# The recurrent block's join on pairs of tiles, output tiles copied by ScalarE, and a norm's squares summed by TensorE

## The reference

```python
def rmsnorm(x, g):
    y = xf * lax.rsqrt(jnp.mean(xf * xf, axis=-1, keepdims=True) + RMS_EPS)
    return (y * g).astype(x.dtype)

for i in range(DEPTH):                       # DEPTH = 2
    a = rmsnorm(h, g[0])
    m = retention_mixer(a, ...) if i % 2 == 0 else rglru_mixer(a, ...)
    h = h + rmsnorm(m, g[1])
    f = conv_ffn(rmsnorm(h, g[2]), ...)
    h = h + rmsnorm(f, g[3])

def rglru_mixer(h, ...):
    gate, xr = jnp.split(h @ w_in, 2, axis=-1)
    xr = dwconv(xr, conv_w, conv_b, LRU_CONV_LEFT)
    y = (rglru_one_direction(xr, ..., False) + rglru_one_direction(xr, ..., True))
    y = y * jax.nn.gelu(gate)
    return y @ w_out
```

## Time and profile before

| | us |
|---|---|
| median of three runs | 717.61 |
| the profiled execution, its own time | 717.85 |
| its span on the profile | 716.0 |
| TensorE busy (matmul) | 704.6 |
| VectorE busy | 607.3 |
| ScalarE busy | 520.2 |
| GpSimd busy | 25.0 |

### The profile page before, as it was taken

One profiled execution on the slowest core, in us unless ns is written; L12 is line 12 of the kernel. 1 busy time (PEld: TensorE's weight loads), 2 busy tenths in 40 slices (PEclk: granted clock), 3 DMA queues, 4 the chain that ended last, 5 costly groups with the idle time before them and its releaser, 6 DMA issues.

```text
span 716.0 us, 16121 instructions
## 1 busy us (share of the span) xinstructions
PE 704.6 (98%) x6542; PEld 589.9 (82%) x6542; DVE 607.3 (85%) x820; ACT 520.2 (73%) x848; POOL 25.0 (3%) x28
## 2 busy tenths in 40 slices
PE   9999999999999999999999999999899999999996
PEld 6788787878899888888889998888788888885464
DVE  6969877777889799989898889898999999999643
ACT  7566675857576789778777677899668888988431
POOL 0010010101010000000002300000000000000000
PEclk9999999999999999999999999999999999999999
DMA  9873363452683356555589963100525666766821
GB/s 309 318 234 120 119 235 119 166 188 104 211 274 121 111 192 225 192 195 200 176 264 388 370 216 117 62 1 1 196 98 190 224 206 207 233 211 207 275 43 59
DMA packets 106396, 132.08 MB, mean 184 GB/s; under 512 B 12385, under 2 KB 74337, under 8 KB 106209
## 3 DMA queue, kind: packets, MB, share of 16 engines
q1 hardware_dynamic: 105904, 130.97, 54.4%
q10 hardware_dynamic: 432, 0.31, 0.2%
HBM read 129.17 MB, written 1.05 MB: 182 GB/s over the span
## 4 chain that ended last, share of the span: by engine, by line
PE 82%; DVE 8%; ACT 6%; DMA 2%; issue 1%; SPq 1%; DVEq 0%
PE ps L1653 22%; PE ps L1655 22%; PE ps L1654 22%; PE ps L2036 3%; PE ps L2037 3%; PE ps L2035 3%; DMA stage<-in_ret_w_in 2%; PE ps L1696 1%; PE ps L1700 1%; PE ps L1695 1%; DVE a_lo L1082 1%; SPq L495 1%; PE ps L1901 1%; DVE hT L1098 1%; DVE w_lo L1036 1%
## 5 line engine op out<-in xcount | busy, mean ns | idle before, releaser
L1653 PE MATMUL ps<-a_hi,w_hi 128*128 128x272 f16 (+1 forms) x1000 | 276.9, 277 | 0.1
L1654 PE MATMUL ps<-a_lo,w_hi 128*128 128x272 f16 (+1 forms) x1000 | 276.9, 277 | 0.0
L1655 PE MATMUL ps<-a_hi,w_lo 128*128 128x272 f16 (+1 forms) x1000 | 276.9, 277 | 0.0
L1036 DVE SCALAR_TENSOR_TENSOR w_lo<-stage,w_hi 128x1024 f16<-128x1024 f32 x207 | 246.5, 1221 | 34.3 <-ACT w_hi L579 34.0
L579 ACT ACTIVATE w_hi<-stage 128x1024 f16<-128x1024 f32 x207 | 208.5, 1044 | 30.6 <-PE ps L2037 18.3
L1653 PEld LDWEIGHTS ps<-a_hi,w_hi 128*128 128x128 f16 x1000 | 97.8, 98 | 17.3 <-DVE rs L1045 0.9
L1655 PEld LDWEIGHTS ps<-a_hi,w_lo 128*128 128x128 f16 x1000 | 97.8, 98 | 16.0
L1654 PEld LDWEIGHTS ps<-a_lo,w_hi 128*128 128x128 f16 x1000 | 97.8, 98 | 15.7
L1653 PE MATMUL ps<-y_hi,w_hi 128*128 128x272 f16 (+3 forms) x496 | 106.1, 242 | 0.0
L1654 PE MATMUL ps<-y_lo,w_hi 128*128 128x272 f16 (+3 forms) x496 | 106.1, 242 | 0.0
L1655 PE MATMUL ps<-y_hi,w_lo 128*128 128x272 f16 (+3 forms) x496 | 106.0, 242 | 0.0
(11 more groups left out here) (278 smaller groups left out, 1104.2 us busy)
## 6 DMA issues: line engine op xcount, KB each, us to landing
stage<-in_ffn_w_in SPq DMA_DIRECT2D x96, 512.0 KB
stage<-in_ffn_w_out SPq DMA_DIRECT2D x24, 1024.0 KB
stage<-in_ret_w_in SPq DMA_DIRECT2D x16, 1024.0 KB
stage<-in_ret_w_out SPq DMA_DIRECT2D x8, 1024.0 KB
stage<-in_lru_w_in SPq DMA_DIRECT2D x8, 1024.0 KB
stage<-in_ret_w_in SPq DMA_DIRECT2D x12, 512.0 KB
stage<-in_lru_w_out SPq DMA_DIRECT2D x8, 512.0 KB
stage<-in_lru_w_a SPq DMA_DIRECT2D x8, 256.0 KB
```

Of the source, the lines that this page charges most:

```text
L1036: dve.scalar_tensor_tensor(out=part(1, c, q), in0=flat(stage, c, q), scalar=W_SCALE, in1=part(0, c, q), op0=ALU.mult, op1=ALU.subtract).th ...
L1653: pe.matmul(o, w_h, x_h, start=start, stop=False)
L1654: pe.matmul(o, w_h, x_l, start=False, stop=False)
L1655: return pe.matmul(o, w_l, x_h, start=False, stop=stop)
```

## The change

It has three parts.

First, ScalarE now copies all eight output tiles of the recurrent block with their gain from PSUM into `mT` (`out_scaled`), between and behind the squares. VectorE's `out_scale` for tiles 0 and 1 is gone there. `mean_part` waits for the first of these copies (`m_part`) where it waited for `m_scaled`.

Second, `residual` takes its tiles in plain order and in groups: tile 0, tile 1, then the pairs (2, 3), (4, 5), (6, 7). One VectorE instruction multiplies a whole group by the root, one adds it to h. The low parts are still made tile by tile, behind the addition of the next group. `norm_input` and `chunk_normed` follow in plain order.

Third, in the join before the recurrent block (`residual_parts` with i = 1), VectorE stops its sums of squares with four tiles left (0, 1, 4, 5), and TensorE multiplies all four with the ones in `mean_input`.

```diff
-JOIN_ORDER = (2, 3, 0, 1, 4, 5, 6, 7)
+GROUPS = ((0, 1), (1, 1), (2, 2), (4, 2), (6, 2))
...
             def norm_input(i, t0, weights_after=()):
-                for n, dt in enumerate(JOIN_ORDER):
-                    act.wait_ge(h_new, (i - 1) * DT + n + 1)
+                for dt in range(DT):
+                    act.wait_ge(h_new, (i - 1) * DT + dt + 1)
                     high(i, dt, t0)
...
+            def out_scaled(half, n):
+
+                act.activation(mT[:, half * 4 + n, T0_LRU_OUT:T], ps[:, (X, Y)[half] + n, T0_LRU_OUT:T], ACTF.Copy,
+                               scale=gain(5, half * 4 + n)).then_inc(m_part, 1)
+
             out_squares(LRU_OUT + 1, 2, 0, T0_LRU_OUT, 2)
-            out_squares(LRU_OUT + 1, 2, 1, T0_LRU_OUT)
+            out_scaled(0, 0)
+            out_scaled(0, 1)
+            out_square(LRU_OUT + 1, 2, 1, 0, T0_LRU_OUT)
+            out_scaled(0, 2)
+            out_square(LRU_OUT + 1, 2, 1, 1, T0_LRU_OUT)
+            out_scaled(0, 3)
+            out_square(LRU_OUT + 1, 2, 1, 2, T0_LRU_OUT)
+            out_square(LRU_OUT + 1, 2, 1, 3, T0_LRU_OUT)
+            for n in range(3):
+                out_scaled(1, n)
             estimate(STAT, T0_LRU_OUT, ms_up, MEAN[("post", 2)], ESTIMATE[("post", 2)])
+            out_scaled(1, 3)
             norm_input(3, T0_LRU_OUT, (4, 6))
...
             def out_scale(i, t0):
-                for dt in range(4 if i < 2 else 2):
+                for dt in range(4):
...
             def residual_parts(i):
...
-                mark(dve.tensor_tensor(two, two, sq[:, 2:4, :], ALU.add))
+                added = mark(dve.tensor_tensor(two, two, sq[:, 2:4, :], ALU.add))
                 part_low(i, 1, 3)
+                after(added)
                 dve.wait_ge(h_sq, (i + 2) * DT)
-                link(dve.tensor_tensor(four, four, sq[:, 6:8, :], ALU.add))
-                link(dve.tensor_tensor(two, two, four, ALU.add))
-                dve.tensor_tensor(sq_sum[:], sq[:, 0, :], sq[:, 1, :], ALU.add).then_inc(sum_h, 1)
+                if i == 1:
+                    dve.tensor_tensor(four, four, sq[:, 6:8, :], ALU.add).then_inc(sum_h, 1)
+                else:
+                    link(dve.tensor_tensor(four, four, sq[:, 6:8, :], ALU.add))
+                    link(dve.tensor_tensor(two, two, four, ALU.add))
+                    dve.tensor_tensor(sq_sum[:], sq[:, 0, :], sq[:, 1, :], ALU.add).then_inc(sum_h, 1)
...
             def residual(i, t0):
                 rsqrt(rs, STAT, t0, ESTIMATE[("post", i)])
-                dve.wait_ge(m_scaled, i + 1)
-                for n in range(DT + 1):
-                    if n < DT:
-                        dt = JOIN_ORDER[n]
-                        to = mT[:, dt, t0:T]
-                        if dt < 2:
-                            link(dve.tensor_tensor(to, to, rs[:, t0:T], ALU.mult))
-                        else:
-                            link(dve.scalar_tensor_tensor(out=to, in0=ps[:, (X, Y)[dt // 4] + dt % 4, t0:T],
-                                                          scalar=gain(2 * i + 1, dt), in1=rs[:, t0:T],
-                                                          op0=ALU.mult, op1=ALU.mult))
-                        dve.tensor_tensor(hT[:, dt, t0:T], hT[:, dt, t0:T], to, ALU.add).then_inc(h_new, 1)
-                    if n:
-                        norm_low(i + 1, n - 1, JOIN_ORDER[n - 1], t0)
+                for g in range(len(GROUPS) + 1):
+                    if g < len(GROUPS):
+                        dt, count = GROUPS[g]
+                        some = slice(dt, dt + count)
+                        dve.wait_ge(m_part, i * DT + dt + count)
+                        link(dve.tensor_tensor(mT[:, some, t0:T], mT[:, some, t0:T],
+                                               rs[:, t0:T].unsqueeze(1).to_broadcast([P, count, T - t0]), ALU.mult))
+                        dve.tensor_tensor(hT[:, some, t0:T], hT[:, some, t0:T], mT[:, some, t0:T],
+                                          ALU.add).then_inc(h_new, count)
+                    if g:
+                        before_dt, count = GROUPS[g - 1]
+                        for dt in range(before_dt, before_dt + count):
+                            norm_low(i + 1, dt, dt, t0)
...
-            out_scale(2, T0_LRU_OUT)
             prep(LRU_OUT + 2, 2)
             prep(LRU_OUT + 2, 3)
             residual(2, T0_LRU_OUT)
...
             def chunk_normed(c, i, t0):
-                for at, k in enumerate(JOIN_ORDER):
-                    if at % 2 == 0:
-                        pe.wait_ge(wlo_made, SUB * c + max(k // 2, 1) + 1)
-                    pe.wait_ge(ahi_made, NORM_BASE[i] + at + 1)
+                for k in range(KC):
+                    if k % 2 == 0:
+                        pe.wait_ge(wlo_made, SUB * c + k // 2 + 1)
+                    pe.wait_ge(ahi_made, NORM_BASE[i] + k + 1)
                     for n in range(4):
-                        if (at, n) == (0, 3):
-                            pe.wait_ge(h_new, (i - 1) * DT + 2)
...
-                    pe.wait_ge(alo_made, NORM_BASE[i] + at + 1)
+                    pe.wait_ge(alo_made, NORM_BASE[i] + k + 1)
...
                 def issue():        # in mean_input
+                    elif i == 2:
+                        for dt in (0, 1, 4, 5):
+                            mm = pe.matmul(ps[:, STAT_IN[i], :T], ones_sb[:, 0, :], sq[:, dt, :], start=dt == 0, stop=dt == 5)
+                        mm.then_inc(ms_up, 1)
...
             def mean_part(i, t0, dt, start=False):
                 if start:
-                    pe.wait_ge(m_scaled, i + 1)
+                    pe.wait_ge(m_part, i * DT + 1)
```

More of the change, by code:

```diff
@@ L597, in norm_input @@
             def norm_input(i, t0, weights_after=()):
-                for n, dt in enumerate(JOIN_ORDER):
-                    act.wait_ge(h_new, (i - 1) * DT + n + 1)
+                for dt in range(DT):
+                    act.wait_ge(h_new, (i - 1) * DT + dt + 1)
                     high(i, dt, t0)
                     act.activation(sq[:, dt, t0:T], hT[:, dt, t0:T], ACTF.Square).then_inc(h_sq, 1)
-                    if n in weights_after:
-                        prep(FFN1_IN + 1, weights_after.index(n))
+                    if dt in weights_after:
+                        prep(FFN1_IN + 1, weights_after.index(dt))
             def norm_tokens():
@@ L1059, in out_scale @@
             def out_scale(i, t0):
-                for dt in range(4 if i < 2 else 2):
+                for dt in range(4):
                     dve.wait_ge(m_sq, i * DT + dt + 1)
-                    last = dve.tensor_scalar(mT[:, dt, t0:T], ps[:, (FULL + [X])[i] + dt, t0:T], gain(2 * i + 1, dt), None,
+                    last = dve.tensor_scalar(mT[:, dt, t0:T], ps[:, FULL[i] + dt, t0:T], gain(2 * i + 1, dt), None,
                                              ALU.mult)
@@ L1738, in chunk_normed @@
                 wh, wl = weights(c)
-                for at, k in enumerate(JOIN_ORDER):
-                    if at % 2 == 0:
-                        pe.wait_ge(wlo_made, SUB * c + max(k // 2, 1) + 1)
-                    pe.wait_ge(ahi_made, NORM_BASE[i] + at + 1)
+                for k in range(KC):
+                    if k % 2 == 0:
+                        pe.wait_ge(wlo_made, SUB * c + k // 2 + 1)
+                    pe.wait_ge(ahi_made, NORM_BASE[i] + k + 1)
                     for n in range(4):
-                        if (at, n) == (0, 3):
-                            pe.wait_ge(h_new, (i - 1) * DT + 2)
                         col = slice(n * P, (n + 1) * P)
-                        pe.matmul(ps[:, X + n, t0:T], wh[:, k, col], a_hi[:, k, t0:T], start=at == 0, stop=False)
+                        pe.matmul(ps[:, X + n, t0:T], wh[:, k, col], a_hi[:, k, t0:T], start=k == 0, stop=False)
                         pe.matmul(ps[:, X + n, t0:T], wl[:, k, col], a_hi[:, k, t0:T], start=False, stop=False)
-                    pe.wait_ge(alo_made, NORM_BASE[i] + at + 1)
+                    pe.wait_ge(alo_made, NORM_BASE[i] + k + 1)
                     for n in range(4):
                         mm = pe.matmul(ps[:, X + n, t0:T], wh[:, k, n * P:(n + 1) * P], a_lo[:, k, t0:T],
-                                       start=False, stop=at == KC - 1)
-                    if at == 3:
-                        mm.then_inc(w_used, 2)
-                    elif at > 3 and at % 2:
+                                       start=False, stop=k == KC - 1)
+                    if k % 2 == 1:
                         mm.then_inc(w_used, 1)
```

## The result

The changed kernel took 719.82 us (median of 14 runs, 719.53 to 720.83), the kernel before, in 14 runs beside it, 718.00. The ratio is 1.0025 [1.0017, 1.0034]: 1.8 us slower (1.2 to 2.4). The profiled execution took 720.04 us with a span of 718.3, against 717.85 and 716.0 before, so the difference of the two is 2.19. The granted clock is full speed in both.

What follows compares the result with a forecast made beforehand. TensorE and, in the recurrent block, ScalarE were taken to bound the kernel, so delays at both places add: 0.74 + 0.44 = +1.18 us on the median 717.61 gives 718.8 us, range 717.6 to 719.9.

Steps and rivals of the forecast that it cites:

- no measurable change: Whole kernel: time between 716.2 and 719.0 us, within 0.2% of the kernel before; chance 0.64.
- Place A: Sum of squares ahead of the recurrent block: three more TensorE products, 1.35 us, make the first gate matmul 0.74 later.
- the whole 1.35 is paid: Rival ahead of the recurrent block: TensorE meets the same 0.6 us wait behind XR1, giving 719.4 us; chance 0.18.
- swallowed: Rival: ScalarE's 0.66 us wait at its recurrent-block run takes most of the 0.74, giving 718.1 us; chance 0.08.
- Copies hidden: Join behind the recurrent block: ScalarE's copies hide behind the mean's sums; last square ends 515.57, wanted at 516.54.
- Start of the MLP: Behind the recurrent block: TensorE starts the MLP's first chunk 0.16 us earlier, at 520.64 instead of 520.80.
- Low parts: MLP's first chunk: pairs delay low parts of tiles 1 and 2, gaps 0.19 and 0.41; chunk ends 0.44 us later.
- Place A and B together: Sum of the costs ahead of and behind the recurrent block: 0.74 + 0.44 = +1.18 us.
- the term for all that follows place B: Behind the MLP's first chunk: VectorE is ahead of its old times, so nothing new is late; no cost.
- place B: The change's place behind the recurrent block: copies, first tile and low parts, forecast to end the MLP's first chunk +0.44 us.
- VectorE is the bound: Rival at both places: two dropped additions and the pairs make the kernel 2.6 us faster, 715.0 us; chance 0.04.

Runs made afterwards that it cites:

- e7_pe_only: Kernel before plus three unused TensorE ones-products in chunk XR1, behind the reading of the root: 718.84 us against 717.95, ratio 1.0013.
- e8_root_only: Kernel before plus three idle ScalarE estimates ahead of the real one, so the root is late: 718.54 us against 717.95, ratio 1.0005.
- e3_join_singles: Kernel before plus ScalarE's copies and plain tile order, with eight single tiles in place of pairs: 717.72 us against 718.21, ratio 0.9995.
- e11_pad4: Changed kernel plus four useless VectorE memsets in its wait ahead of the recurrent block: 719.35 us against 718.05 for the kernel before, ratio 1.0019.
- before_again: The kernel before, unchanged, traced a second time: one execution of 718.88 us.
- after_again: The changed kernel, unchanged, run again (the repeat): 720.50 us (5 runs) against 718.00 for the kernel before, ratio 1.0036.
- e2_join: Kernel before plus the change's first two parts only, sum of squares left on VectorE: 718.86 us against 718.21, ratio 1.0013.

## Why the prediction came out as it did

The time on record was 718.8 with a range of 717.6 to 719.9; the medians were 719.82 and, in the repeat, 720.50. The likeliest case in my chances was no measurable change, and the kernel is slower by 0.25%, just over the bound; the first interval still holds 0.2%, the repeat's (0.22% to 0.50%) does not. The mechanisms at both places were right and their sizes nearly; what was missing is a third term, at the end. That 719.82 lies inside the range is in part luck: the upper edge came from a rival that turned out wrong, 719.82 is 0.1 below it, and the repeat's 720.50 is above it.

- *Place A, forecast +0.74:* measured +0.76 or 0.77. Both chains came as worked out up to the gate; e7_pe_only and e8_root_only show each alone. The four products took 0.46 each, not 0.45. The rival "the whole 1.35 is paid" is out, since the root's chain kept its distance; "swallowed" is out as well, since ScalarE's 0.66 us wait stood unchanged.
- *Copies hidden:* right. The last square was taken at 516.37 at the latest (515.63 + 0.74), and the mean's products ran without a gap. The spacings in the forecast were too long: two copies follow each other by 0.36 (513.66 to 514.38 for two, where 0.42 was assumed) and squares by 0.27 (four in 1.22, the last about 0.40); the 0.33 read from rows 6 had a wait for TensorE in it. e3_join_singles shows the copies at no cost.
- *Start of the MLP, forecast -0.16:* measured -0.22 or -0.23. The products of the mean were 0.08 us shorter as a row too: the first step took 0.22 us, as all the others, where it had taken 0.29. Why was not tried.
- *Low parts, forecast gaps 0.19 and 0.41:* measured 0.17 and 0.48, chunk +0.67 instead of 0.60. Two terms were off and partly cancelled. A linked product over a pair took 0.80 to its addition (522.39 to 523.19), where I took 0.72 from two additions; and TensorE used the low part 0.06 us after its end, where I had 0.15 from a high part by ScalarE.
- *Place A and B together, forecast +1.18:* measured +1.20 (e11_pad4 starts XR1 at 434.61, as the kernel before did at 434.60, and ends the chunk at 532.56 against 531.36).
- *The step that failed:* the term for all that follows place B, put at nothing: "Behind it VectorE is ahead of its old times ... so nothing new is late". In work this is true; yet the last root came 0.37 us later. I had taken it that fewer instructions on an engine cannot cost time elsewhere. What the runs showed in its place: a delay that stays at record 1088 of VectorE's stream, and a shorter stream that moves the last root onto it.
- *Where the number stood:* 1.20 + 0.37 = 1.57, inside the measured 1.8 (1.2 to 2.4) and at the lower edge of the repeat's 2.6 (1.6 to 3.6). Both medians lie above 1.57; whether that is the spread of executions or something that the distances miss is open. On the 718.0 that the kernel before took beside it, the forecast's +1.18 gives 719.2. The remaining 0.4 in my number is that three runs of before had given 717.61.

The rival "VectorE is the bound" had the two dropped additions and the pairs as a gain of 2.6 us. VectorE's work did shrink (607.3 to 604.8 us busy), its time on the path did not: at place A it came 1.2 us sooner and then stood waiting for 1.87.

The trace has a product over a pair at 0.69 us and two single ones at 0.42 or 0.43 each, so a joined instruction saves 0.15 us of busy time (2 x 0.42 - 0.69). The Trainium skill (page "VectorE: DVE Perf Modes", section on the TRN2 errata) has, beside the 58 cycles of its table, (N + 151)/0.96 ns for an fp32 addition of two tensors, measured at N of 512 and 2048. By it an addition takes an estimated 0.43 us for 258 and 0.69 us for 516 elements; this case's trace agrees (0.43 and 0.70). It is busy time only: in e3_join_singles, without the pairs, the chunk was 0.67 us shorter (10.55 against 11.22).

## What to carry to other kernels

Joining instructions on an engine that feeds another piece by piece saves its busy time and delays its first pieces; count when each piece is wanted, not the sum. A wait on the receiving engine tells how much added work it absorbs, but the other chain that ends at the same instruction has to be worked out as well, since both may bind within hundredths. Compare traces by distances from a common point behind the last late load, since the absolute times differ by over 1 us for reasons of their own. And follow the chain to its last instruction even where the change touches nothing: fewer instructions on an engine moved a delay of 0.37 us onto the path, 180 us behind the change.

## What the runs showed of the hardware

**A stall that belongs to a place in VectorE's stream.** One instruction near the end starts late (by 0.27 us at L1572, 0.37 at a root) with nothing to wait for. Which one it is depends on what stands ahead of it in the stream: it is VectorE's record 1088, recorded semaphore waits included, in all nine traces that show it. One 8 KB transfer of an instruction queue (q14) comes close to it: 0.65 or 0.66 us after the start of the late instruction in eight of the nine (708.34 in the kernel before), 0.93 in the changed kernel's first trace (714.22). In the five traces without a gap it lies between 0.41 before and 0.30 after the start of record 1088 (e11_pad4: 709.59, beside two long products, L1591, from 708.63). The DMA view of the changed kernel, 712 to 716 us, in 40 slices of 0.1, and the queue's line:

```profile
GB/s 389 451 226 41 0 0 0 0 0 0 0 0 0 0 0 0 0 0 0 0 0 0 82 0 0 0 0 0 0 0 0 0 0 0 0 0 0 0 0 123
...
q14 instruction: 1, 0.01, 0.5%
```

It is the slice with 82 GB/s. The late instruction starts before this transfer does, so it did not wait for its data. That the two have one cause (the next block of VectorE's instructions) fits the traces; it was not shown, since no run changes the one without the other, and at other transfers of this queue (606.6 and 646.7 in the kernel before, for instance) VectorE has long instructions and no gap.

**The length of a product over a pair.** It lasts 0.69 us like an addition over a pair, but its linked successor starts 0.80 after it, three times of three (0.79 or 0.80), where behind the addition it is 0.72. Behind each product over a pair the trace has a semaphore wait of its own as a record (523.12 for the product at 522.39), and behind the additions of rows 8 none. Whether that makes the 0.08 was not tried.

**The spread between executions.** XR1 started within 3.6 us (433.82 to 437.37) in the traces, and what lies behind it kept its distances to 0.03 us. The differences arise in the first 35 us, at 214 us (the changed kernel's first trace) and at 418 us (before_again, after_again, e2_join, e3_join_singles).
